# A two-block network on one core: products of zeros in the first stage, half of x scaled before the first split, column tiles in p·V, and reordered queues in four layers

## Chip, core and metric

One core of a Trainium2 chip runs the whole program. The metric is the device time of one execution in microseconds (us), the median of the runs. A profiled execution of the same program gives the trace.

## What is computed

The input x has 256 tokens of 1024 values. A first block and a second block follow each other; every product is of float32 weights with float32 activations. Cut to what matters (`rms_norm_2` is `rms_norm`; rope, gates and residuals are left out where they change nothing in the order of the work):

```python
def first_block(x, ...):
    f = (silu(rms(h) @ w1) * (rms(h) @ w3)) @ w2            # ffn1, width 2816
    h = h + 0.5 * rms_norm(f, ffn1_post_g)
    proj = rms_norm(h, mix_pre_g) @ w_in                    # mix: 10 blocks of columns
    y_a = dsa_attention(q_a, k_a, v_a, q_i, k_i, w_i) @ w_a_out     # 8 heads of 64
    y_b = (gate_b * short_conv_causal(gate_c * conv_in, conv_w)) @ w_b_out
    h = h + rms_norm((sigmoid(g_a) * y_a + sigmoid(g_b) * y_b) @ w_out, mix_post_g)
    h = h + rms_norm(memory_cross_attention(...), xattn_post_g)
    h = h + 0.5 * rms_norm(swiglu(...), ffn2_post_g)        # ffn2
def second_block(x, ...):
    x = x + rwkv7_time_mix(rms_norm(x), ...)                # xx = shift(h) - h; xs = h + xx * mu; r, k, v = xs @ w
    x = x + square(relu(rms_norm(x) @ w1)) @ w2             # mlp1, width 4096
    k, v = shared_kv(x)
    x = x + swa_sink_attention(q, k, v, sinks) @ wo         # window attention, 16 heads of 64
    x = x + square(relu(rms_norm(x) @ w1)) @ w2             # mlp2
```

## The kernel before, in words

The 256 tokens are two tiles of 128 ("token 0" and "token 1" below, `NT` = 2). Activations are kept as columns: a pair of buffers (`XA`, `XB` or `MID`), one with the high and one with the low half of each value. A weight chunk of 128 × 1024 values is loaded by SyncE (SP) into one of six raw slots; ScalarE (ACT) writes its high half (`split_hi`, L263, or L266 where a gain is multiplied in), VectorE (DVE) its low half (`split_lo`, L279 or L282), and TensorE (PE) makes three products of 128 × 128 × 512 for each pair (`product`, L290 to L292: high·high, low·high, high·low). The semaphores `hi_done`, `lo_done` and `chunk_used` tie them: a load waits for the low half that last used its raw slot, a high half waits for the products that last used its split slot. Each engine has one queue, in which the order of all this is written out by hand; `split_hi(A, n)` and `split_lo(V, n)` issue all splits up to chunk n at that place of the queue, and an instruction behind one that waits, waits too.

The layers run one after the other: ffn1, mix, xattn (memory attention), ffn2, time mixing (`tmix`), mlp1, window attention (`window`), mlp2. The feed-forward layers are loops over blocks of their width, with a tail (`pe_tail`) in which the two token tiles go apart, so that the next layer can begin (`follow`).

The places that the change touches:

- *First stage.* `setup.pe` (L1096) waits for the constants and one gain, and transposes the gain (L1099). `pre.turn.pe_token` (L452) transposes x of a token in two groups of four. ACT (`act_token`, L459) and DVE (`dve_token`, L466) write its eight high and eight low columns with the gain multiplied in; `act_deferred` and `dve_deferred` issue the first split ahead of them (`split=1`). A product of chunk m waits for the low half of the chunk and for columns up to 2m + 1. SP issues four chunks, x of token 1 between them, then two chunks that wait for the low halves of chunks 0 and 1, then the small vectors and the constants (L1082 to L633), then the next chunks.
- *p·V.* In `Mix.pe_values` (L1289) and `WindowAttention.pe_values` (L3430) each head's probabilities (128 × 128, plain float32) are the stationary side and 64 columns of values the moving one. A plain float32 call issues two matmuls. `COLUMN_TILES` doesn't exist yet; products that write to half of the partitions are used in the time mixing (L2765, L2813, L2816; L2732 to L2791 use a half of the rows too).
- *Mix.* ACT's exponentials (`act_exp`, L1435) of token 1 are behind `split_hi(A, c[9] + 3)`; the activations before them are sigmoids. In DVE's queue `dve_merge(V, 1)` (L1658) stands behind `split_lo(V, out[1] + 2)`; PE's transposes of the merged rows (L506) wait for it.
- *ffn2's tail and the entry of the time mixing.* `pe_h_turn` (L2417) multiplies h by a diagonal that holds the norm (ACT, L2402). `pe_mixed` starts with the two groups of token 0. ACT: `ffn2_post.act(A, 1)` (Square of the accumulator of token 1, L406), `act_h_cols` (L2284), `act_hi_part` (L2316). DVE: `dve_xx_part` (L2298, L2295), `dve_xs_part` (L2307), `dve_lo_part` (L2312), and between them `ffn2_post.dve_scale` (L656) and `dve_add` (L661). `pe_r_token` waits for the low part of its token and half.
- *Window.* `window.act` and `window.dve` (from L3549 and L3661) interleave the splits with turning h into columns (`act_wide` L487, `dve_wide` L491), the norms, the squares and sums of q (L3513, L3596), q rows (L3604), bias, max and exponentials of four units u (kv group, token), p columns (L3540), o rows (L3654), and the high and low half of o (L3547, L3659). GpSimd (POOL) makes the reciprocal roots (L419, L3364). `WindowAttention.pe` writes out the order of PE: products of q and kv, transposes of q rows (L3398), logits (L3410), transposes of p (L3420), values (L3430), transposes of o (L3439) and the output products (`pe_out`).

## Time and profile before

| | us |
|---|---|
| median of 3 runs | 1415.51 |
| lowest of the runs | 1413.01 |
| the profiled execution: device time | 1416.03 |
| the profiled execution: span of its core | 1414.3 |

In the profile PE is the matmul stream of TensorE and PEld its weight loads, which overlap it; DVE is VectorE, ACT ScalarE, POOL GpSimd, SP SyncE, and SPq SyncE issuing DMAs. A line number is that of the instruction in the kernel; where a helper issues it, that of the helper. "128\*64" behind an operation is rows × columns of the stationary side. A trace can lack a few per cent of the matmul records.

### The profile page before, as it was taken

What the parts mean: (1) busy time and instruction counts of PE and PEld (TensorE: products, weight loads), DVE (VectorE), ACT (ScalarE), POOL (GpSimd) and SP (SyncE); (2) the same over time, 40 slices, a digit from 0 to 9 for tenths busy, and PEclk for the clock granted to TensorE, in tenths of its full rate; (3) what the DMA queues carried; (4) which work ended last, traced back from release to release, by engine and by line L of the source; (5) the groups of instructions that cost most, each with busy time, mean ns of one, the idle gap of its engine ahead of it and who ended that gap; (6) DMA issues with size and microseconds to landing.
All of it is one profiled execution on the core that took longest, in us unless ns stands there. A gap on an engine that the chain in (4) does not pass through costs nothing.

```text
span 1414.3 us, 23277 instructions
## 1 busy us (share of the span) xinstructions
PE 1366.0 (97%) x8675; PEld 1119.8 (79%) x8675; DVE 855.1 (60%) x1235; ACT 697.4 (49%) x1109; POOL 37.7 (3%) x41
## 2 busy tenths in 40 slices
PE   7999999999999999999899999899999988999998
PEld 5888877878788878888677688678888877788887
DVE  4545568875655464455865688656555576565554
ACT  5444456665465554444544453235444456454442
POOL 0000000000000000000000000100000020000000
PEclk9999999999999999999899999999999999999999
DMA  8655546555445565555443100315555641265553
GB/s 290 218 178 178 178 142 209 165 177 194 155 158 161 154 218 192 179 178 179 142 164 98 38 3 32 111 60 179 180 186 184 225 150 45 75 199 188 182 189 104
DMA packets 145534, 220.51 MB, mean 156 GB/s; under 512 B 16760, under 2 KB 65166, under 8 KB 145328
## 3 DMA queue, kind: packets, MB, share of 16 engines
q1 hardware_dynamic: 145456, 219.43, 47.4%
q8 instruction: 54, 0.88, 0.3%
q14 instruction: 24, 0.20, 0.1%
HBM read 218.33 MB, written 1.05 MB: 155 GB/s over the span
## 4 chain that ended last, share of the span: by engine, by line
PE 87%; DVE 6%; ACT 3%; issue 1%; DMA 1%; POOL 1%; SPq 1%; ACTq 0%; DVEq 0%; POOLq 0%
PE acc L290 12%; PE gp L290 12%; PE acc L292 12%; PE acc L291 12%; PE gp L292 12%; PE gp L291 12%; PE gp L2732 1%; PE tp L929 1%; PE acc L2747 1%; DVE sb_w_lo L279 1%; DMA sb_raw<-in_ffn_w 1%; ACT sb_w_hi L263 1%; PE acc L1255 1%; PE tp L290 1%; PE tp L292 1%
## 5 line engine op out<-in xcount | busy, mean ns | idle before, releaser
L279 DVE TENSOR_TENSOR sb_w_lo<-sb_raw,sb_w_hi 128x1024 fp32r<-128x1024 f32 (+1 forms) x380 | 451.7, 1214 | 217.0 <-ACT sb_w_hi L263 215.1
L263 ACT ACTIVATE sb_w_hi<-sb_raw 128x1024 fp32r<-128x1024 f32 (+1 forms) x380 | 388.2, 1053 | 218.2 <-PE acc L292 107.2
L290 PE MATMUL gp<-sb_w_hi,sb_xa_hi 128*128 128x512 f32 (+1 forms) x752 | 301.0, 400 | 11.6 <-DVE sb_xa_lo L2312 6.4
L292 PE MATMUL gp<-sb_w_lo,sb_xa_hi 128*128 128x512 f32 (+1 forms) x752 | 293.8, 391 | 0.0
L291 PE MATMUL gp<-sb_w_hi,sb_xa_lo 128*128 128x512 f32 (+1 forms) x752 | 293.2, 390 | 0.0
L290 PEld LDWEIGHTS gp<-sb_w_hi,sb_xa_hi 128*128 128x128 f32 x752 | 142.5, 190 | 45.3 <-DVE sb_w_lo L279 8.2
L292 PEld LDWEIGHTS gp<-sb_w_lo,sb_xa_hi 128*128 128x128 f32 x752 | 142.4, 189 | 30.1
L291 PEld LDWEIGHTS gp<-sb_w_hi,sb_xa_lo 128*128 128x128 f32 x752 | 142.9, 190 | 27.6 <-issue 0.5
L290 PE MATMUL acc<-sb_w_hi,sb_mid_hi 128*128 128x512 f32 x400 | 156.2, 390 | 0.0
L292 PE MATMUL acc<-sb_w_lo,sb_mid_hi 128*128 128x512 f32 x400 | 155.8, 389 | 0.0
L291 PE MATMUL acc<-sb_w_hi,sb_mid_lo 128*128 128x512 f32 x400 | 155.6, 389 | 0.0
L796 DVE SCALAR_TENSOR_TENSOR sb_arena<-gp,sb_stat,sb_arena 128x256 f32<-128x256 f32 x44 | 19.6, 479 | 131.2 <-ACT sb_arena L773 131.2
L290 PE MATMUL acc<-sb_w_hi,sb_xa_hi 128*128 128x512 f32 (+1 forms) x240 | 95.0, 396 | 3.5 <-DVE sb_w_lo L282 2.0
L773 ACT ACTIVATE sb_arena<-gp,sb_stat 128x256 f32<-128x256 f32 x44 | 18.9, 471 | 148.4 <-PE gp L292 148.4
L292 PE MATMUL acc<-sb_w_lo,sb_xa_hi 128*128 128x512 f32 (+1 forms) x240 | 91.9, 383 | 0.0
L291 PE MATMUL acc<-sb_w_hi,sb_xa_lo 128*128 128x512 f32 (+1 forms) x240 | 91.7, 382 | 0.0
L292 PEld LDWEIGHTS acc<-sb_w_lo,sb_mid_hi 128*128 128x128 f32 x400 | 75.1, 188 | 15.7
L291 PEld LDWEIGHTS acc<-sb_w_hi,sb_mid_lo 128*128 128x128 f32 x400 | 75.1, 188 | 15.4
L290 PEld LDWEIGHTS acc<-sb_w_hi,sb_mid_hi 128*128 128x128 f32 x400 | 75.1, 188 | 15.4
L290 PEld LDWEIGHTS acc<-sb_w_hi,sb_xa_hi 128*128 128x128 f32 x240 | 45.1, 188 | 14.4 <-issue 3.4
L290 PE MATMUL acc<-sb_w_hi,sb_xb_hi 128*128 128x512 f32 x128 | 52.2, 408 | 3.4 <-DVE sb_xb_lo L3659 3.4
L292 PEld LDWEIGHTS acc<-sb_w_lo,sb_xa_hi 128*128 128x128 f32 x240 | 45.1, 188 | 9.1
(409 smaller groups left out, 1751.7 us busy)
## 6 DMA issues: line engine op xcount, KB each, us to landing
sb_raw<-in_ffn_w SPq DMA_DIRECT2D x264, 256.0 KB, 4.3
sb_raw<-in_mlp_w SPq DMA_DIRECT2D x256, 256.0 KB, 2.9
sb_raw<-in_w_in SPq DMA_DIRECT2D x72, 256.0 KB, 3.0
sb_raw<-in_a_w_rkv SPq DMA_DIRECT2D x48, 256.0 KB, 4.3
sb_raw<-in_xattn_w_kv SPq DMA_DIRECT2D x32, 256.0 KB, 3.5
sb_raw<-in_w_out SPq DMA_DIRECT2D x16, 256.0 KB, 2.9
sb_raw<-in_xattn_w_q SPq DMA_DIRECT2D x16, 256.0 KB, 2.9
sb_raw<-in_xattn_w_o SPq DMA_DIRECT2D x16, 256.0 KB, 3.0
```

Source lines behind the costliest of these rows:

```text
L263: A.e.activation(w_hi[:, s, :, 0:n], raw[:, r, :, 0:n], ACT.Copy).then_inc(hi_done, 1)
L279: V.e.tensor_tensor(w_lo[:, s, :, 0:n], raw[:, r, :, 0:n], w_hi[:, s, :, 0:n].bitcast(F32), ALU.subtract).then_inc(lo_done, 1)
L290: e.matmul(dst, xh, wh, start=start, stop=False)
L291: e.matmul(dst, xl, wh, start=False, stop=False)
L292: return e.matmul(dst, xh, wl, start=False, stop=stop)
L773: A.e.activation(self.silu[:, t, 0:256], gp[:, t, 0:256], ACT.Silu, scale=self.norm.st[:, t:t + 1]).then_inc(self.acted, 1)
L796: V.e.scalar_tensor_tensor(self.mid_rows[:, t, 0:256], gp[:, t, 256:512], self.norm.st[:, t:t + 1], self.silu[:, t, 0:256], ALU.mult, ALU. ...
L929: mm = T.e.transpose(tp[:, b, (2 * j + t) * P:(2 * j + t + 1) * P], self.mid_rows[:, t, at:at + P], ident)
L1255: mm = T.e.matmul(self.side(n)[:, j * self.KEYS[t]:(j + 1) * self.KEYS[t]], q, kk, start=True, stop=True)
L2732: mm = T.e.matmul(gp[there, s, m * HALF:(m + 1) * HALF], self.mt[s][at, m, 0, there], self.x_inv[s][at, m, :], start=True, stop=True)
L2747: mm = T.e.matmul(acc[at, s, 512:1024][:, at_m], self.y_inv[s][there, m, :], self.z_buf[s][there, m, :], start=True, stop=True)
```

## The change

One `Exp` of a single column is added, memsets and products of zeros are added in the first stage, `pe_enter` is cut off `pe_mixed` and issued inside ffn2's tail (`follow`, `late=1`), p·V is issued in two column halves, and the rest is a new order of the same instructions. The diff, with the lines around the changes left out:

```diff
@@ -73,6 +73,7 @@
 HALF = P // 2
+COLUMN_TILES = (slice(0, HALF), slice(HALF, P))
@@ -414,7 +415,7 @@
             def pool_token(self, G, t):
-                    G.e.wait_ge(half_ready, 1)
+                    G.e.wait_ge(half_ready, 2)
                     G.e.wait_ge(self.mean, self.count(t))
@@ -452,15 +453,15 @@
-            def act_token(self, A, t, *targets):
-                for k in range(self.kts):
+            def act_token(self, A, t, *targets, ks=None):
+                for k in range(self.kts) if ks is None else ks:
                     A.e.wait_ge(self.turned, self.turned0 + 2 * t + k // 4 + 1)
...
-            def dve_token(self, V, t, *targets):
-                for k in range(self.kts):
+            def dve_token(self, V, t, *targets, ks=None):
+                for k in range(self.kts) if ks is None else ks:
                     V.e.wait_ge(self.hi, self.hi0 + 4 * self.sets * (2 * t + k // 4 + 1))
@@ -577,8 +578,13 @@
                     before0()
-                split_hi(A, first + split)
-                self.turn.act_token(A, 0, *self.targets)
+                if split == 1:
+                    self.turn.act_token(A, 0, *self.targets, ks=range(0, KT // 2))
+                    split_hi(A, first + split)
+                    self.turn.act_token(A, 0, *self.targets, ks=range(KT // 2, KT))
+                else:
+                    split_hi(A, first + split)
+                    self.turn.act_token(A, 0, *self.targets)
                 if before1 is not None:
@@ -592,8 +598,13 @@
                     before0()
-                split_lo(V, first + split)
-                self.turn.dve_token(V, 0, *self.targets)
+                if split == 1:
+                    self.turn.dve_token(V, 0, *self.targets, ks=range(0, KT // 2))
+                    split_lo(V, first + split)
+                    self.turn.dve_token(V, 0, *self.targets, ks=range(KT // 2, KT))
+                else:
+                    split_lo(V, first + split)
+                    self.turn.dve_token(V, 0, *self.targets)
                 if before1 is not None:
@@ -882,7 +893,7 @@
-            def pe_tail(self, T, follow):
+            def pe_tail(self, T, follow, late):
@@ -899,9 +910,11 @@
                     self.columns_ready(T, 1)
+                    if late:
+                        self.pe_down_token(T, i, 1, range(late))
                     if follow is not None:
                         follow()
-                    self.pe_down_token(T, i, 1, range(self.tiles))
+                    self.pe_down_token(T, i, 1, range(late, self.tiles))
                 else:
@@ -939,10 +952,11 @@
-            def pe(self, T, pre, h_ready, acc_free=None, aside=None, turned=True, follow=None):
+            def pe(self, T, pre, h_ready, acc_free=None, aside=None, turned=True, follow=None, late=0):
...
                     pre.turn.pe_token(T, 0, h_rows, h_ready(0))
+                    setup.pe_warm(T, 12)
                 self.pe_up_token(T, 0, 0, range(0, 3), pre.turn)
@@ -961,7 +975,7 @@
                     self.pe_turn(T, i)
-                self.pe_tail(T, follow)
+                self.pe_tail(T, follow, late)
@@ -1094,6 +1108,8 @@
             def pe(self, T):
+                T.e.wait_ge(half_ready, 1)
+                self.pe_warm(T, 8)
                 T.e.wait_ge(consts_loaded, 16)
@@ -1126,7 +1142,15 @@
+            def warm(self):
+                return rows(3)[:, 0, 0:P]
+
+            def pe_warm(self, T, n):
+                for _ in range(n):
+                    T.e.matmul(acc[:, 0, 0:P], self.warm(), self.warm(), start=True, stop=True)
+
             def pool(self, G):
+                G.e.memset(self.warm(), 0.0).then_inc(*G.one(half_ready))
                 G.e.memset(half[:, :], -0.5).then_inc(*G.one(half_ready))
@@ -1286,8 +1310,9 @@
                     for c in range(t + 1):
-                        mm = T.e.matmul(self.side(t)[:, head * HD:(head + 1) * HD], self.p_cols[t][:, c, head, :], self.values[:, c, :],
-                                        start=c == 0, stop=c == t)
+                        for at in COLUMN_TILES:
+                            mm = T.e.matmul(self.side(t)[at, head * HD:(head + 1) * HD], self.p_cols[t][:, c, head, at], self.values[:, c, :],
+                                            start=c == 0, stop=c == t)
                 mm.then_inc(*T.one(self.o))
@@ -1516,7 +1541,9 @@
                 self.act_taken(A, 7, lambda t: rows(5)[:, t, 512:1024], ACT.Sigmoid)
+                A.e.activation(self.sums[:, 8:9], ident[:, 0:1], ACT.Exp).then_inc(*A.one())
                 split_hi(A, c[9] + 3)
+                A.e.wait_ge(*A.last)
                 self.act_exp(A, 1, 0)
@@ -1734,7 +1761,6 @@
                 self.dve_gate_a(V, 1, self.ya1, lambda t: gp[:, t, :])
-                split_lo(V, out[1] + 2)
                 self.dve_merge(V, 1)
@@ -2344,20 +2370,21 @@
                 ffn2_post.dve_mean(V, 1)
+                self.dve_xx_part(V, 0, 1)
+                self.dve_lo_part(V, 0, 0)
                 ffn2_post.dve_scale(V, 1)
-                self.dve_lo_part(V, 0, 0)
                 V.e.wait_ge(*V.last)
                 ffn2_post.dve_add(V, 1)
-                self.dve_xx_part(V, 0, 1)
+                self.dve_xs_part(V, 0, 1)
                 self.pre.rms.dve(V, 1)
-                self.dve_xs_part(V, 0, 1)
                 split_lo(V, r.first[0] + 3)
...
                 split_lo(V, r.first[0] + 4)
-                for g in range(2):
-                    self.dve_xx_part(V, 1, g)
-                    self.dve_xs_part(V, 1, g)
+                self.dve_xx_part(V, 1, 0)
+                self.dve_xs_part(V, 1, 0)
+                self.dve_xx_part(V, 1, 1)
                 self.dve_lo_part(V, 1, 0)
+                self.dve_xs_part(V, 1, 1)
                 self.dve_lo_part(V, 1, 1)
@@ -2444,9 +2471,11 @@
-            def pe_mixed(self, T):
+            def pe_enter(self, T):
                 self.pe_h_turn(T, 0, 0)
                 self.pe_h_turn(T, 0, 1)
+
+            def pe_mixed(self, T):
                 self.pe_r_token(T, 0, 0)
@@ -3427,8 +3456,9 @@
                     for c in range(t + 1):
-                        mm = T.e.matmul(self.o_bank(u)[:, head * HD:(head + 1) * HD], self.p_col[u][:, c, head, :],
-                                        self.kv_rows[:, c, P + kv * HD:P + (kv + 1) * HD], start=c == 0, stop=c == t)
+                        for at in COLUMN_TILES:
+                            mm = T.e.matmul(self.o_bank(u)[at, head * HD:(head + 1) * HD], self.p_col[u][:, c, head, at],
+                                            self.kv_rows[:, c, P + kv * HD:P + (kv + 1) * HD], start=c == 0, stop=c == t)
                 mm.then_inc(*T.one(self.o))
@@ -3439,12 +3469,12 @@
-            def pe_out(self, T, b, t, n):
+            def pe_out(self, T, b, t, n, ms=range(2)):
...
                     T.e.wait_ge(*((self.q_rows, t + 1) if n == 0 else stage(self.o_rows, t + 1)))
-                for m in range(2):
+                for m in ms:
                     c = self.out_first + 4 * b + 2 * n + m
@@ -3493,8 +3523,9 @@
                 self.pe_values(T, 3, (self.o_rows, 3))
-                self.pe_out(T, 1, 0, 1).then_inc(token0_done, 1)
+                self.pe_out(T, 1, 0, 1, range(0, 1))
                 self.pe_turn_o(T, 3, (self.o_done, 3))
+                self.pe_out(T, 1, 0, 1, range(1, 2)).then_inc(token0_done, 1)
                 self.pe_out(T, 1, 1, 0)
@@ -3549,15 +3580,16 @@
                 split_hi(A, self.first + 3)
-                for t in range(NT):
-                    for g in range(2):
-                        self.turn.act_wide(A, t, g, self.entry_bank(t, g), XA)
+                for g in range(2):
+                    self.turn.act_wide(A, 0, g, self.entry_bank(0, g), XA)
                 split_hi(A, self.first + 4)
-                for t in range(NT):
-                    self.rms.act(A, t, h_rows, rows(6)[:, t, :], mlp1_add.h_at(t))
+                self.rms.act(A, 0, h_rows, rows(6)[:, 0, :], mlp1_add.h_at(0))
+                for g in range(2):
+                    self.turn.act_wide(A, 1, g, self.entry_bank(1, g), XA)
+                self.rms.act(A, 1, h_rows, rows(6)[:, 1, :], mlp1_add.h_at(1))
                 split_hi(A, self.kv_first + 2)
                 self.act_squares(A, 0)
-                split_hi(A, q1 + 3)
+                split_hi(A, q1 + 2)
                 self.act_squares(A, 1)
@@ -3578,8 +3610,8 @@
                 split_hi(A, out + 5)
+                self.act_o_hi(A, 1)
                 self.act_p_cols(A, 2)
-                self.act_o_hi(A, 1)
                 self.act_exp(A, 3)
@@ -3667,9 +3699,9 @@
                 mlp1_add.dve(V, 1, mlp1)
+                split_lo(V, self.first + 4)
                 for g in range(2):
                     self.turn.dve_wide(V, 1, g, self.entry_bank(1, g), XA)
-                split_lo(V, self.first + 4)
                 for t in range(NT):
@@ -3677,11 +3709,11 @@
                 split_lo(V, q1 + 1)
+                self.dve_sums(V, 1)
                 self.dve_q_rows(V, 0)
                 split_lo(V, q1 + 2)
-                self.dve_sums(V, 1)
+                self.dve_q_rows(V, 1)
                 split_lo(V, q1 + 4)
-                self.dve_q_rows(V, 1)
                 self.dve_k_sums(V)
@@ -3694,9 +3726,9 @@
                 self.dve_bias(V, 2)
-                split_lo(V, out + 3)
                 self.dve_q_rows(V, 3)
                 self.dve_o_rows(V, 0)
+                split_lo(V, out + 3)
                 self.dve_o_lo(V, 0)
@@ -3838,7 +3870,7 @@
             xattn.pe(T)
-            ffn2.pe(T, ffn2_pre, xattn.post.h_at, xattn.post.freed, None, True)
+            ffn2.pe(T, ffn2_pre, xattn.post.h_at, xattn.post.freed, None, True, lambda: tmix.pe_enter(T), 1)
             tmix.pe_mixed(T)
...
             tmix.pe_core(T)
```

## Rows read from the trace of the kernel before

**Rows 1.** The page: its first line, and the busy time of each engine.
```profile
span 1414.3 us, 23277 instructions
PE 1366.0 (97%) x8675; PEld 1119.8 (79%) x8675; DVE 855.1 (60%) x1235; ACT 697.4 (49%) x1109; POOL 37.7 (3%) x41
```
**Rows 2.** PE's waits, stretches 0:32, 275:365, 675:705, 1130:1225: total, times, longest us.
```profile
PE gp L290 <- DVE sb_xa_lo L466: 3.3, 2, 3.2
...
PE tp L1282 <- ACT sb_arena L1435: 1.6, 1, 1.6
PE tp L506 <- DVE sb_arena L1658: 1.3, 1, 1.3
...
PE gp L290 <- DVE sb_xa_lo L2312: 6.4, 2, 4.5
...
PE acc L290 <- DVE sb_xb_lo L3659: 3.4, 2, 2.0
PE tp L3398 <- DVE sb_arena L3604: 3.3, 2, 1.7
PE acc L290 <- DVE sb_w_lo L282: 2.0, 1, 2.0
```
**Rows 3.** Stretches: length, busy PE PEld DVE ACT POOL (count), clock, DMA, GB/s.
```profile
10.20:12.90 2.70, 2.66 (x6) 1.91 (x7) 2.65 (x8) 2.08 (x3) 0.00 (x0) 1.00 1.10 362
...
29.40:60.00 30.60, 30.60 (x137) 25.01 (x138) 16.34 (x18) 14.41 (x21) 0.00 (x0) 1.00 0.67 220
686.40:692.00 5.60, 5.53 (x14) 4.37 (x15) 4.99 (x12) 2.16 (x4) 0.65 (x1) 0.50 0.83 311
...
699.30:703.00 3.70, 3.70 (x11) 2.92 (x10) 3.44 (x5) 2.37 (x3) 0.00 (x0) 0.54 0.22 70
...
1157.00:1175.00 18.00, 18.00 (x121) 14.77 (x119) 16.05 (x43) 10.88 (x36) 2.99 (x2) 1.00 0.20 68
...
1197.10:1201.50 4.40, 4.32 (x12) 3.43 (x13) 1.43 (x4) 4.25 (x16) 0.00 (x0) 0.61 0.34 106
```
**Rows 4.** The chain that ended last, first stage: start us, us, what.
```profile
8.35 1.22 DVE sb_w_lo L279
9.57 2.07 DVE sb_xa_lo L466 x8
11.64 1.14 DVE sb_w_lo L279
...
18.88 0.66 SPq L240
19.57 7.36 DMA sb_raw<-in_ffn_w
```
**Rows 5.** Timeline of PE, p·V and half-width products: start us, us, engine, line, operation.
```profile
282.64 1.89 PE L1289 MATMUL acc<-sb_arena 128*128 128x64 f32 x16
...
889.01 0.28 PE L2813 MATMUL tp<-sb_arena,sb_shade 128*64 128x64 f32 x4
889.13 0.29 PE L2816 MATMUL tp<-sb_arena,sb_shade 128*64 128x64 f32 x4
...
917.87 0.68 PE L2775 MATMUL acc<-sb_arena,sb_shadow 64*64 64x64 f32 x8
918.47 0.50 PE L290 MATMUL acc<-sb_w_hi,sb_xa_hi 128*128 128x512 f32 x1
```
**Rows 6.** Timeline of ACT, before the exponentials and before the time mixing.
```profile
308.81 1.28 ACT L1435 ACT_TABLE_LOAD   x1
...
678.88 0.40 ACT L2402 ACTIVATE sb_arena<-sb_consts,sb_stat 128x128 f32<-128x128 f32 x1
```
**Rows 7.** The chain that ended last, entry of the time mixing: start us, us, what.
```profile
680.15 0.91 PE tp L2417 x8
...
684.54 1.28 DVE sb_arena L656
...
696.91 1.14 DVE sb_arena L2307 x4
```

## The prediction

> **What bounds the kernel now.** I read the page first: TensorE (PE) is busy 1366.0 of 1414.3 us [rows 1], so nothing that shortens the work of VectorE (DVE), ScalarE (ACT) or a DMA counts unless PE is then waiting for it. Second, PE's waits by stretch [rows 2]: the reader is to see how few there are. The first stage has 3.3 us (longest 3.2), the mix layer 1.6 and 1.3 us, the entry of the time mixing 6.4 us in two waits (longest 4.5), the window layer 3.4 + 3.3 + 2.0 us. The feed-forward loops, most of the span, have none. Third, the pace of PE and its granted clock [rows 3]: undisturbed, 137 products of 512 columns take 30.60 us, 0.223 us each, at clock 1.00. After the waits of the time mixing 14 take 5.60 us at 0.50, and 11 take 3.70 us at 0.54; after one in the window layer 12 take 4.40 us at 0.61. Those are TensorE's two levels, 2.4 and 1.2 GHz, and a wait costs the slow products behind it as well. The stretch 10.2 to 12.9 shows 6 products in 2.70 us, the slow pace, though the row prints a clock of 1.00; I go by the pace. What a new order can win is in these few places.
>
> **The sum is made against the profiled execution**: span 1414.3, device time 1416.03 us. The median of the runs shown is 1415.51, 0.5 lower.
>
> **First stage.** Products of zeros are added (8 before the first transpose, 12 behind token 0's transposes), and ACT and DVE scale half of x before the first split. Before, the chain runs: DVE splits the first chunk from 8.35, makes eight low halves of x from 9.57, and only then splits the second chunk from 11.64; SyncE's issue of a later chunk waits for that split, 13 issues of vectors and constants are behind it in SP's queue, and the chunk issued at 18.88 lands after 7.36 us [rows 4]. PE's stalls around 29 us hang on that landing. With four low halves made before the first raw chunk is split, DVE's 1.22 + 2.07 us of work starts about 0.7 us earlier, so the second split, SP's queue and the landing move by that: −0.7 us. The products of zeros: a plain fp32 product issues two matmuls, 8 + 12 make 40. The first 16 lie under PE's wait for the first DMAs; the other 24 lie between the transposes and the first real product, at 0.11 us each if the clock is up (2.6 us; an estimate from the 0.108 us of L1289 in [rows 5], whose stationary side has the same 128 columns), or twice that if it is not (5.3 us, ending some 2.5 us after the present first product). The memset that they wait for has no row of its size. What the early clock gives, (0.45 − 0.22) × 6 = 1.4 us, is not on the chain that ends last, which is SP's. I take −0.7; bounds −1.5 and +2.
>
> **Column tiles.** p·V in the mix layer (L1289) and the window layer (L3430) is split into two halves of 64 columns. Now 16 such matmuls take 1.89 us, 0.108 us each from start to start; the 24 calls of L1289 and the 48 of L3430 are two matmuls each, 144 in all, 15.6 us [rows 5]. The change makes 288. The same form, 128 rows × 64 columns with 64 moving columns, alternating between the two tiles, stands in the time mixing: four at 889.01, the next at 889.13, 0.029 us each [rows 5]. 288 × 0.029 = 8.4 us, 7.2 less. Entering and leaving a tiled mode: eight matmuls of L2775 at 917.87 hold PE for 0.60 us, against 0.23 at 0.029 each [rows 5]; I take 0.35 for each of the six groups, 2.1 in all (bounds 0 and 0.37 × 6). Net 5.1 us less, of which the two groups in the mix layer, 48 of the 144 with 2 of the 6 switches, are on the path: 5.2 − 2.8 − 0.7 = −1.7 us. The window's share is counted below, without the first group, whose time turns into waiting.
> The Trainium skill (TensorEngine Tiling, "Theoretical Speedup") gives up to 2x where a dimension is at most 64. By it alone the 15.6 us would become 7.8, and the sum would be 0.6 us lower than by the row. Against the change stands the same page's "Key Properties": changing the tiling mode drains TensorE. The 0.60 us row agrees that a switch is not free.
>
> **Mix layer.** The Exp table load of 1.28 us [rows 6] sits in front of the exponentials that PE waits 1.6 us for; a dummy Exp moves it to where ACT waits for PE, one split earlier. ACT's next work there is not needed for two splits: −1.3 us. In the merge, one DVE split (1.22 us, [rows 4] shows one) goes behind the addition that PE waits 1.3 us for; the chunk delayed is three chunks, 8 us of products, ahead of its use: −1.1 us, leaving a rest of 0.2.
>
> **Entry of the time mixing.** The 16 transposing matmuls of token 0 move into the middle of token 1's last 12 down products (6 in front, 6 behind). Now they start at 680.15 by the chain; six products of 0.23 before that is 678.8, but ACT's diagonal is there only at 678.88 + 0.40 [rows 6, 7], so PE waits some 0.5 us there instead. Token 1 of the accumulator is finished 16 × 0.11 + 0.5 = 2.3 us later, and behind it in ACT's queue stands the high half that the first product wants. So I expect the wait of 4.5 us to be cut to about 4.2 by work put into it, and the first product to start at the same time within 0.3 us. The gain comes later: scaling the residual (1.28 us, L656) now stands behind the low part, and the last mix group of token 1 (four of L2307, 1.14 us [rows 7]) now stands behind the low part that PE waits 1.9 us for. About 0.9 us of that wait stays removed after the later start of the residual is taken off. With a wait below 1 us I expect the clock to hold, and 11 products at 0.336 fall to 0.223: 1.2 to 1.6 us. −2.3 us; bounds +2.5 (token 1's delay not hidden) and −4.
>
> **Window layer.** (a) At its entry ACT makes the high half of a chunk and then DVE its low half only after token 1's columns; PE waits 2.0 us. Both orders are turned round, and the chunk is there 4 us before its use: −2.2 with its restart. (b) ACT squares token 1 one split earlier and DVE sums it before it makes q rows 0, so the reciprocal root on GpSimd starts earlier and q rows 1 is there in time: the first of the two L3604 waits goes, −1.9 (the 1.5 and the earlier start of its neighbours). From 1157 to 1175 DVE is busy 16.05 of 18.00 us [rows 3]; it must follow, and every link at its head moves by the same 4.1. (c) A split of 1.22 us [rows 4] leaves the front of q rows 3, of which I take 0.9, because GpSimd's root ends in between; together with the shorter chain to ACT's third p group −1.4. (d) Values 1: 32 matmuls, 3.5 us, become 64, 1.9 + 0.35: −1.2. (e) ACT's high half of o before its p columns, on the chain to the 2.0 us wait: −1.2, and with two waits of 0.6 in place of 2.2 the clock holds, 12 products at 0.367 fall to 0.223: −1.7. (f) Values 2 −0.3, values 3 −1.2. (g) The last output product is cut in two around the transposes of o, so the 1.4 us wait for its low half is under six products: −1.5. Sum 2.2 + 1.9 + 1.4 + 1.2 + 1.2 + 1.7 + 0.3 + 1.2 + 1.5 = 12.6 us. Bounds: 4 (only a and b) and 14 (the waits and slow products of this stretch altogether, plus the tiles).
>
> **Total:** 0.7 + 1.7 + 1.3 + 1.1 + 2.3 + 12.6 = 19.7; 1416.0 − 19.7 = 1396.3, and 1396 against the median.
>
> **The rivals.**
> *The window's second half gives nothing back to PE* (DVE, at 89% from 1157 to 1175, or ACT's exponentials become the wait there). For it: that share. Against it: the waits named are for single links that the new order does shorten. Then only a and b count, 8.5 us less gain: 1405. Chance 0.16.
> *The entry of the time mixing turns worse* because the accumulator of token 1 is late: +2.5 in place of −2.3, 1401. For it: ACT's queue; against: DVE, not ACT, holds the chain at L656. Chance 0.12.
> *More than summed*: the clock also holds at the other two places: 2.5 us at the first wait of the time mixing and 1.3 in the window layer, 1392. Chance 0.08.
> *The column tiles run one behind the other* (the other side). 288 matmuls at the present 0.108 are 31.1 + 2.1 us against 15.6: +17.7; without the tiles' 4.4 the rest of the sum is −15.3, so 1418.4, slower than before. It decides from 0.100 us a matmul. Against it stands the 0.029 row of the same shape. Chance 0.03. A milder form is a floor in PE's sequencer of, say, twice the row, 0.058: 16.7 + 2.1 − 15.6 = +3.2, giving 1404; chance 0.03.
> The Trainium skill (TensorE: Matmul & The Clock Gate, "Wait — 56ns, not 53.3ns?") states such a floor: about 62 ns per MATMUL where hardware decode is off. The 0.029 row speaks against it here; by it the time would be about 1405.
> *The zeros do not lift the clock*: then 24 of them delay the first real product by up to 2.5 us, of which the later waits of that stage take up some; at most +2, 1399, inside the range.
>
> **How the numbers follow.** The forecast has 0.58. Its own width (±4) and the rivals at 1401, 1404 and 1405 are taken in, as is 1392; outside are the slower case and the tails: 1390 to 1408. Two per cent, about what a measurement of this kernel can tell from no change, is 28 us, more than all waits and slow products listed: faster 0.04, slower 0.01, within 0.95.
>
> **What would show it.** The first chunk split on ACT behind four halves of x; products near 10 us at 0.22. L1289 and L3430 with 96 and 192 matmuls at 0.03. No table load in front of the exponentials at 308. L506's wait near 0.2. A wait near 4 us at the entry of the time mixing, the second below 1, clock 1.00 behind it. In the window layer no wait for L282 or before the second L3398; products behind values 1 at clock 1.00. I am wrong if the two window waits reappear under another name, or if the token 1 products of the time mixing start later than now.

## The result, and the profile after

| | before | changed |
|---|---|---|
| median, us | 1415.21 (3 runs, 1413.01 to 1415.51) | 1399.51 (4 runs, 1396.91 to 1400.44) |
| the profiled execution: device time, us | 1416.03 | 1399.79 |
| its span, us | 1414.3 | 1397.6 |

A fourth run of before took 2748.47 us; runs in such a slow state are left out here. The ratio of the times is 0.9894, 95% interval 0.9882 to 0.9906: 1% faster, less than the 2% from which a kernel is called faster here. 1396 was forecast with a range of 1390 to 1408. The median came out 3.5 us above the forecast and inside the range.

The page of the changed kernel, its first line and the busy time, against [rows 1]:

```profile
span 1397.6 us, 23649 instructions
PE 1362.7 (98%) x8859; PEld 1115.1 (80%) x8859; DVE 855.7 (61%) x1235; ACT 697.1 (50%) x1110; POOL 38.1 (3%) x42
```

PE has 184 matmuls more (144 for the halves of p·V, 40 products of zeros) and is still busy 3.3 us less. PE's waits of the changed kernel, stretches 0:32, 275:365, 665:700, 880:915 and 1115:1215 (total, times, longest, us), against [rows 2]:

```profile
PE gp L291 <- DVE sb_w_lo L280: 2.6, 3, 1.4
PE acc L1150 <- POOL sb_half L1154: 1.0, 1, 1.0
...
PE tp L507 <- DVE sb_arena L1685: 0.3, 1, 0.3
PE tp L1306 <- ACT sb_arena L1460: 0.2, 1, 0.2
...
PE gp L291 <- DVE sb_xa_lo L2338: 4.5, 2, 3.6
PE tp L2444 <- ACT sb_arena L2429: 1.7, 2, 1.2
...
PE acc L2747 <- DVE sb_shade L3005: 1.5, 1, 1.5
PE gp L2761 <- issue: 1.0, 1, 1.0
...
PE tp L3427 <- DVE sb_arena L3636: 1.7, 1, 1.7
...
PE tp L3469 <- DVE sb_arena L3686: 0.7, 1, 0.7
PE acc L291 <- DVE sb_xb_lo L3691: 0.5, 1, 0.5
```

The reader is to see: the wait for the exponentials has shrunk from 1.6 to 0.2 and that for the merged rows to 0.3; the wait of 4.5 at the entry of the time mixing is 3.6 now, with a new one of up to 1.2 for ScalarE's diagonal; in the window layer the 2.0 at the entry and one of the two waits for q rows are gone, the other (L3427) stayed at 1.7, and the two waits for the low half of o (3.4 together) have shrunk to one of 0.5. Two lines weren't forecast: a wait of 0.7 for the rows of o (L3469), and a line that I never looked for: 1.0 us that ends on nothing the profile shows, in the core of the time mixing.

Where the gain is, I read by putting the 4704 matmuls of the weight products (512 columns each) in one table, the n-th of before beside the n-th of the other kernel, and taking the difference of their starts. Here are the differences by stretch, for all traces of this study (positive: gained on the first trace of before; places in before's time, us):

| kernel | 0 to 60 | mix layer (to 365) | entry of time mixing (670 to 706) | its core (706 to 930) | window layer (1110 to 1225) | in all |
|---|---|---|---|---|---|---|
| forecast | 0.7 | 4.1 | 2.3 | 0 | 12.6 | 19.7 |
| changed | −0.5 | 4.4 | 2.4 | −1.5 | 11.9 | 16.6 |
| changed_again | 0.1 | 4.3 | 2.4 | −3.0 | 12.3 | 16.2 |
| before_again | 0.4 | 0.0 | 2.8 | 0.2 | 1.6 | 5.0 |
| first_before | 0.6 | 4.4 | 2.4 | −3.4 | 11.8 | 15.9 |
| half_only | 0.9 | 4.4 | 2.4 | −2.3 | 11.9 | 17.3 |
| zeros_only | −0.4 | 4.4 | 2.4 | 0.3 | 12.3 | 18.9 |
| values_in_one | −2.1 | 2.5 | 2.4 | −2.8 | 9.8 | 9.9 |
| window_before | −2.3 | 4.4 | 2.4 | −0.5 | 4.1 | 8.1 |
| entry_before | −0.7 | 4.4 | 3.0 | 0.1 | 10.2 | 16.9 |
| paced | −0.2 | 4.4 | 2.5 | 1.1 | 11.8 | 19.5 |
| best_new_entry | 0.9 | 4.4 | 2.4 | −1.8 | 12.4 | 18.3 |
| best_old_entry | 0.2 | 4.3 | 3.0 | −0.6 | 11.9 | 18.7 |
| mixed_entry | 0.8 | 4.4 | 3.7 | −0.6 | 11.9 | 20.0 |

The row of before_again is the same program as before, traced a second time. It is 5.0 us faster, 4.4 of them in two stretches of the table. That row is why the experiments were needed: a gain read from one pair of traces is partly the luck of the pair.

### The profile page after: what moved, and what is told of

Its sections match the earlier page's. It is cut to its first block, busy times and chain, and to the rows that moved or that the text cites. A ratio compares the mean times of both kernels' runs of the same rounds, so it can differ in the third digit from the quotient of the medians.

```text
span 1397.6 us, 23649 instructions
## 1 busy us (share of the span) xinstructions
PE 1362.7 (98%) x8859; PEld 1115.1 (80%) x8859; DVE 855.7 (61%) x1235; ACT 697.1 (50%) x1110; POOL 38.1 (3%) x42
## 4 chain that ended last, share of the span: by engine, by line
PE 87%; DVE 6%; ACT 3%; issue 1%; DMA 1%; POOL 1%; SPq 0%; POOLq 0%; ACTq 0%; DVEq 0%
PE acc L291 12%; PE acc L293 12%; PE acc L292 12%; PE gp L291 12%; PE gp L293 12%; PE gp L292 11%; PE gp L2761 2%; PE tp L942 1%; PE acc L2776 1%; DVE sb_w_lo L280 1%; DMA sb_raw<-in_ffn_w 1%; ACT sb_w_hi L264 1%; PE acc L1279 1%; PE tp L291 1%; ACT sb_arena L407 1%
## 5 line engine op out<-in xcount | busy, mean ns | idle before, releaser
L280 DVE TENSOR_TENSOR sb_w_lo<-sb_raw,sb_w_hi 128x1024 fp32r<-128x1024 f32 (+1 forms) x380 | 451.8, 1215 | 207.3 <-ACT sb_w_hi L264 205.7
L784 ACT ACTIVATE sb_arena<-gp,sb_stat 128x256 f32<-128x256 f32 x44 | 18.9, 471 | 148.4 <-PE gp L293 148.4
```

The source lines that it names most:

```text
L280: V.e.tensor_tensor(w_lo[:, s, :, 0:n], raw[:, r, :, 0:n], w_hi[:, s, :, 0:n].bitcast(F32), ALU.subtract).then_inc(lo_done, 1)
L784: A.e.activation(self.silu[:, t, 0:256], gp[:, t, 0:256], ACT.Silu, scale=self.norm.st[:, t:t + 1]).then_inc(self.acted, 1)
```

## Experiments

**First stage: first_before, half_only, zeros_only.** The edits, from the changed kernel; first_before makes both, half_only the first alone, zeros_only the second alone:

```diff
-                G.e.memset(self.warm(), 0.0).then_inc(*G.one(half_ready))
-                self.pe_warm(T, 8)
-                    setup.pe_warm(T, 12)
```
```diff
-                if split == 1:
-                    self.turn.act_token(A, 0, *self.targets, ks=range(0, KT // 2))
-                    split_hi(A, first + split)
-                    self.turn.act_token(A, 0, *self.targets, ks=range(KT // 2, KT))
-                else:
-                    split_hi(A, first + split)
-                    self.turn.act_token(A, 0, *self.targets)
+                split_hi(A, first + split)
+                self.turn.act_token(A, 0, *self.targets)
...
```

> The changed kernel with its first stage put back: no memset and no products of zeros, all eight halves of x behind the first split. In the changed kernel the chunk that PE stalls on near 29 us was issued 0.6 us earlier (18.29 for 18.88) and still landed 0.49 us later (27.45 for 26.96), while the DMA engines' share was 0.96 to 1.00 from 20 us on in both. Theory: from 20 us on that stage is bound by the DMA engines and not by the issue, so neither the half of x nor the zeros give anything after 29 us: 1399.0 (0.5 below the changed kernel's 1399.5), first product behind the stall at 29.3. Rival: the issue does set the landing, and the 8.43 us of that one trace was chance: then the old first stage costs the forecast 0.7, 1400.2, product at 30.4 or more. On the side: 40 fewer instructions in PE's queue move the place of the 0.96 us gap at 895.35 (which ends on nothing that the profile shows). If the half clock behind it (898 to 901.5, 1.4 us) hangs on that place, it goes or moves here, and the time is up to 1.4 lower still.

> The changed kernel without its products of zeros (L1150, 16 + 24 matmuls) and their memset; half of x stays in front of the first split. So far: with both parts PE's first products behind the chunk that lands at 27 us start 0.49, 0.74, 0.62 and 0.83 us later than before, and in two of the four traces another 1.46 us is lost between 29.4 and 60 us; with neither part they start 0.60 us earlier than before. Theory: the earlier issue for x-half crowds the DMA queue (the chunk shares it with 0.95 MB of later ones in place of 0.55), so this kernel loses as with both: product near 29.8, time near the changed kernel's. Rival: the zeros do it (their memset, or 40 instructions more to be fetched ahead of PE's first loads): then the product starts 0.6 us before the old 29.33, as with neither, and the time is 1.1 us below the changed kernel's if nothing else moves. In the core of the time mixing 40 instructions fewer put the gap that ends on nothing where first_before has it (2.83 us and 5.6 us of half clock): there it should come out again, since it depends on the count of PE's instructions, so that the total is 1.5 to 2 us above the first-stage forecast.

> The changed kernel with its products of zeros but all eight halves of x behind the first split, as before. Theory (the half of x crowds the queue): product behind the stall near 28.7 to 29.3, no loss. Rival (the zeros do it): product at 29.8 or later. The first six products should run at 0.23 us each in either case, starting near 10.2, since the zeros lift the clock; and the first real product must not be later than before by more than 0.1.

Measured: 1400.69 us (ratio 0.9903, 0.9886 to 0.9920), 1399.20 (0.9891, 0.9868 to 0.9915) and 1399.90 (0.9900, 0.9875 to 0.9924): by time they can't be told apart. The traces tell them apart. The chain that ended last, first stage, of the changed kernel (start us, us, what), against [rows 4]:

```profile
7.79 1.13 DVE sb_xa_lo L467 x4
8.92 1.13 DVE sb_w_lo L280
10.05 1.04 DVE sb_xa_lo L467 x4
11.09 1.14 DVE sb_w_lo L280
...
18.29 0.66 SPq L241
18.99 8.43 DMA sb_raw<-in_ffn_w
```

Up to the issue this pair of traces shows what was forecast: the second split 0.55 us earlier, the issue 18.29 for 18.88. The transfer then takes 8.43 us for 7.36 and eats it. The same line in half_only, and then in zeros_only:

```profile
18.67 7.42 DMA sb_raw<-in_ffn_w
```
```profile
19.22 8.17 DMA sb_raw<-in_ffn_w
```

Over all traces: seven with the zeros take 8.17 to 8.79 us for this transfer, those without them 7.36 to 7.78 (six traces whose chain shows it). So the zeros do it, with the half of x in front or not: of half_only and zeros_only the theory was wrong and the rival right. (For first_before neither held: its product behind the stall starts at 28.7 us, forecast 29.3 or 30.4 and later.) The half of x is shown less clearly: with it the issue is at 17.77 to 18.31 (ten traces, mean 18.1), without it at 18.25 to 18.88 (four traces, mean 18.5), but the two traces of before alone, one program, are 0.49 us apart (18.88 and 18.39). What the zeros bring is there too, the first six products in 1.40 us for 2.66 (timeline of PE, changed kernel: idle time before a group in brackets):

```profile
7.06 2.90 PE L1150 MATMUL acc<-sb_arena 128*128 128x128 f32 x24
10.11 0.50 PE L291 MATMUL gp<-sb_w_hi,sb_xa_hi 128*128 128x512 f32 x1
...
12.27 0.50 PE L291 MATMUL gp<-sb_w_hi,sb_xa_hi 128*128 128x512 f32 x1 [0.51 <-DVE sb_w_lo L280]
```

but PE then waits for splits: at 15 us zeros_only stands about where first_before does, 0.6 and 0.7 us behind the first trace of before. How can 40 products of zeros slow a transfer ten microseconds later? They are 80 instructions of PE (a matmul and a weight load each). DMA queues of the changed kernel, and of half_only, 22 to 24 us (packets, MB, share of 16 engines):

```profile
q1 hardware_dynamic: 177, 0.60, 89.8%
q8 instruction: 1, 0.02, 3.0%
```
```profile
q1 hardware_dynamic: 188, 0.57, 85.9%
```

In every trace with the zeros the first packet of 16 KB of instructions starts between 22.5 and 24.9 us, inside the stretch in which the engines are full with chunks; in every trace without, it comes at 32.4 to 33.4 us, when the chunk has landed. In all fourteen it starts when PE has started 204 to 226 matmuls and weight loads, with the zeros or without: it is PE's own, and the zeros bring PE to that number some 9 us sooner. 3.0% of 16 engines over 2 us is 0.96 us of one engine, and if a chunk counts as landed only with its last part, the delay of one engine is that of the chunk. The size fits the delay of 0.8 to 1.4 us (against 7.36). That the packet comes with the zeros is shown; that it is the packet which delays the chunk, and not something else about the zeros, is argued from the size alone and wasn't tried. In two of the seven, where the wait behind the transfer was longest (1.8 and 1.9 us for 1.3 to 1.6), the clock then fell to 0.50 from 31 to 34 us, which is another 1.46 us lost in values_in_one and window_before.

**p·V in one piece.** 

```diff
-                        for at in COLUMN_TILES:
-                            mm = T.e.matmul(self.side(t)[at, head * HD:(head + 1) * HD], self.p_cols[t][:, c, head, at], self.values[:, c, :],
-                                            start=c == 0, stop=c == t)
+                        mm = T.e.matmul(self.side(t)[:, head * HD:(head + 1) * HD], self.p_cols[t][:, c, head, :], self.values[:, c, :],
+                                        start=c == 0, stop=c == t)
...
```

> The changed kernel with p.V in one piece again (L1313 and L3460: 144 matmuls on 128 columns for 288 on 64). Theory, by the terms of the sum: 1.7 us in the mix layer, 1.2 for values 1, 0.3 and 1.2 for values 2 and 3 come back, 4.4 in all: 1403.9. Rival: only the mix layer's part (trace of the changed kernel: 1.95 us) is on the path, and in the window layer PE waits a little later anyway: 1401.5. Of the half clock behind the gap at 895.35: 96 fewer instructions ahead of it (48 in the mix layer) move it as well; if it hangs on the place it changes here, if it hangs on the 1.49 us wait at 886.6 it stays.

Measured: 1405.91 us, 0.9938 (0.9921 to 0.9956), 2.0 above the theory. In the trace the mix layer loses 1.9 and the window layer 2.1 us against the changed kernel: 4.0, the theory's 4.4 but for the clock. The rest is the two stretches of the table that have nothing to do with p·V: −1.6 in the first stage and −1.3 in the core. Timeline of PE of the changed kernel, against [rows 5]:

```profile
283.18 1.15 PE L1314 MATMUL acc<-sb_arena 128*64 128x64 f32 x32
320.61 2.08 PE L1314 MATMUL acc<-sb_arena 128*64 128x64 f32 x64
...
1177.61 2.09 PE L3460 MATMUL acc<-sb_arena 128*64 128x64 f32 x64
```

About 0.2 of the 2.08 us is the length of the last matmul, so the 64 start 0.030 us apart (an estimate). 16 matmuls at 0.108 and 32 at 0.029 differ by 0.80 us and 0.53 was gained; 32 and 64 differ by 1.60 and 1.38 was gained: by this estimate going over to the half width and back costs 0.2 to 0.3 us (0.35 was taken).

**The window layer's order.**

```diff
-                self.dve_sums(V, 1)
                 self.dve_q_rows(V, 0)
                 split_lo(V, q1 + 2)
-                self.dve_q_rows(V, 1)
+                self.dve_sums(V, 1)
                 split_lo(V, q1 + 4)
+                self.dve_q_rows(V, 1)
...
```
(and likewise the entry, q rows 3, o of unit 1 and the last output product)

> The changed kernel with the window layer's queues put back (entry, q rows 0 and 1, q rows 3, o of unit 1 behind the p columns, last output product in one piece); p.V stays in two halves. Theory: of the 11.8 us that the traces show for the layer the halves of p.V bring 2.7 (1.2 + 0.3 + 1.2), the order 9.1: 1408.6. Rival: order and halves are worth much more together than apart, since a wait that stays long lets the clock fall whatever ran ahead of it: then the order alone is worth all 11 to 12, 1411.

Measured: 1408.07 us, 0.9950 (0.9931 to 0.9969), by the number what the theory says (1408.6). In part that is luck: in its trace 1.8 us are lost in the first stage and 1.0 won in the core against the changed kernel, where nothing was edited. Its waits, 1120 to 1220:

```profile
PE acc L291 <- DVE sb_xb_lo L3689: 3.4, 2, 2.0
PE tp L3427 <- DVE sb_arena L3634: 2.6, 1, 2.6
PE acc L291 <- DVE sb_w_lo L283: 2.0, 1, 2.0
```

In the trace the order is worth 11.9 − 4.1 = 7.8 us, and not 9.1: window_before keeps 2.1 us of gain between 1197.2 and 1203.3, though its wait of 2.0 us is back. There the first trace of before has half clock ([rows 3], 0.61), and neither window_before nor before_again has. And it loses 0.95 us just before, of which more below. before_again, clock of the 4.3 us behind its wait of 2.02:

```profile
1193.70:1198.00 4.30, 4.26 (x25) 3.72 (x26) 1.40 (x3) 4.22 (x16) 0.00 (x0) 1.00 0.33 103
```

**The entry of the time mixing: entry_before and before_again.** entry_before puts back the place of the transposes and VectorE's order:

```diff
-            ffn2.pe(T, ffn2_pre, xattn.post.h_at, xattn.post.freed, None, True, lambda: tmix.pe_enter(T), 1)
+            ffn2.pe(T, ffn2_pre, xattn.post.h_at, xattn.post.freed, None, True)
...
-                self.dve_xx_part(V, 0, 1)
-                self.dve_lo_part(V, 0, 0)
                 ffn2_post.dve_scale(V, 1)
+                self.dve_lo_part(V, 0, 0)
...
```

> The changed kernel with the entry of the time mixing put back (transposes of token 0 of h behind the last down products, old order of VectorE's pieces). Theory: the entry is worth what the two traces show between 678 and 706 us, 2.25 us, and the loss of 1.4 us between 894 and 906 has nothing to do with it: 1401.8, with the second wait on L2338 back near 1.9 us and the granted clock near 0.5 behind it. Rival: the entry moved the phase of everything behind it and so brought the loss; then the loss goes with it: 1400.4.

> The kernel before, unchanged, for a second trace. In entry_before the code of the entry is that of before, and yet 3.0 us of gain appear between 670 and 706 us: half clock for 3.3 us behind the first wait and none behind the second, where the first trace of before has 7.6 and 3.6 us. If the length of such a stretch is a matter of the single execution, this second trace shows other lengths than 7.6 and 3.6, and the same for the 0.80 us gap at 900.3. If it belongs to the program (its timing up to there is the same each time), they come again within 0.3 us.

Measured: entry_before 1399.10 us, 0.9889 (0.9872 to 0.9906), no slower than the changed kernel, where the theory had 1401.8 and the rival 1400.4. Both its waits are those of before, and the clock isn't. Waits 670 to 705 and two stretches (clock is the third number from the end):

```profile
PE gp L291 <- DVE sb_xa_lo L2338: 6.5, 2, 4.5
...
682.90:686.00 3.10, 3.10 (x8) 2.48 (x9) 2.53 (x6) 1.15 (x2) 0.38 (x1) 0.52 1.04 385
693.70:697.40 3.70, 3.67 (x16) 3.06 (x17) 3.37 (x4) 3.44 (x5) 0.00 (x0) 1.00 0.10 22
```

before_again (one run, 1411.03 us) shows the same, 1.00 behind its second wait of 1.9 us:

```profile
697.10:700.80 3.70, 3.70 (x16) 3.07 (x17) 3.43 (x4) 3.43 (x4) 0.00 (x0) 1.00 0.09 22
```

So behind equal waits of 1.9 us the clock fell in one trace (0.54, [rows 3]) and held in three (best_old_entry too). Against those three the new entry gains nothing: 2.4 us in all nine traces that have it, where the old one has 2.8, 3.0 and 3.0. The Trainium skill (TensorE: Matmul & The Clock Gate, "What's actually happening") says that the window in which the clock's monitor looks at the engine runs freely and doesn't start with the kernel. The two traces of before agree with it as far as they go: the same program, behind the same wait, fell in one (0.54) and not in the other (1.00). What phase it had no trace shows.

**Paced loads.** One line, at the end of SP's queue of the time mixing:

```diff
                 for c in range(self.out.first[0] + 6, self.out.end):
                     load_chunk(sp, c)
+                sp.wait_ge(self.y_done, 2 * self.GROUPS - 1)
```

> The changed kernel with one wait more in SP's queue: the first eight loads of mlp1 (2 MB) wait until the last but one group of y of the time mixing is in its rows (about 901 us), in place of being issued from 887.7 on. In all six traces PE has one gap here that ends on nothing the profile shows (0.68 to 2.83 us), and in each a packet of instructions of 16 KB starts 1.5 to 2.7 us before the gap's end, 9.5 us after the one before it, where others are 4 to 5 us apart; in between the DMA engines' share is 0.9 to 1.0 with these loads. Theory: PE's instructions are fetched behind the loads; without them the gap goes, the packets come 4 to 5 us apart, and the clock holds between 897 and 902: 1399.5 - 0.96 - 1.4 = 1397.1. Rival: the gap has another cause (it stays, 1399.5), or the 1.49 us wait before it is what lets the clock fall (gap gone, half clock stays: 1398.5). Against it: the loads, now 13 us later, might come late for mlp1's first products near 930.

Measured: 1397.78 us, 0.9882 (0.9858 to 0.9906), 1.7 below the changed kernel (2.4 were expected). The two weren't timed side by side and their ranges overlap (1396.60 to 1399.08 against 1396.91 to 1400.44), so the time alone shows nothing. The trace does: the gain of the core is 1.1 in place of −1.5. What the changed kernel has there, timeline of PE and clock:

```profile
894.91 0.44 PE L2761 MATMUL gp<-sb_shadow,sb_shade 64*64 64x64 f32 x7
896.31 0.45 PE L2761 MATMUL gp<-sb_shadow,sb_shade 64*64 64x64 f32 x9 [0.96 <-issue]
...
888.00:895.30 7.30, 6.93 (x223) 6.23 (x224) 5.34 (x15) 1.91 (x5) 0.00 (x0) 1.00 0.96 328
898.00:901.60 3.60, 3.60 (x59) 3.44 (x56) 2.05 (x4) 0.38 (x1) 0.00 (x0) 0.53 0.02 6
```

and the waits of paced from 880 to 912, with no such line:

```profile
PE acc L291 <- DVE sb_xa_lo L492: 1.5, 1, 1.5
PE acc L2748 <- DVE sb_shade L3006: 1.5, 1, 1.5
```

PE is at 61 instructions per us before the gap (223 matmuls, 224 loads in 7.3 us), a block of 256 in 4.2 us, and the packets of 16 KB come about that far apart, 4 to 5 us. Around the gap they don't. The DMA queues of the changed kernel from 884.6 to 893.6 us, and from 893.7 to 894:

```profile
q1 hardware_dynamic: 1187, 2.48, 81.4%
...
q1 hardware_dynamic: 53, 0.10, 97.8%
q8 instruction: 1, 0.02, 20.2%
```

Nine microseconds without a packet of instructions, while SP's twelve loads hold the engines at 0.96 (888 to 895.3), and the gap ends 2.3 us behind the start of the late one (893.97). In paced the two packets start at 883.87 and 891.08, 7.2 us apart and not 9.7. Two more things tie the gap to PE's fetches. In all thirteen traces that have it, it ends 2.3 to 2.6 us behind the start of the late packet, whatever its length. And counted from the start of the program it begins each time behind the 12466th or the 12722nd of PE's matmuls and weight loads, which are 256 apart, in kernels whose instructions in front of it differ by up to 176. (best_old_entry has one more such gap, 0.42 us ending at 832.3, behind the 9650th, eleven times 256 sooner.) The Trainium skill (Runtime: NRT & Kernel Launch, "Instruction fetch mechanics") has blocks of 16 KiB and 256 instructions, which these packets bear out, and calls the cost of crossing one mostly hidden: here it isn't, at 0.5 to 2.8 us a time, with 3.4 or 6.8 us of half clock behind it in six of the thirteen traces.

**Together: best_new_entry, best_old_entry, mixed_entry, changed_again.** All four were timed side by side. The first three have no zeros and the paced loads; the second has the old entry, the third this mixture:

```diff
-            ffn2.pe(T, ffn2_pre, xattn.post.h_at, xattn.post.freed, None, True, lambda: tmix.pe_enter(T), 1)
+            ffn2.pe(T, ffn2_pre, xattn.post.h_at, xattn.post.freed, None, True)
...
             def pe_mixed(self, T):
+                self.pe_enter(T)
```

> The changed kernel without its products of zeros and with the paced loads of mlp1. The traces so far: six with the zeros have the transfer that PE stalls on in the first stage at 8.17 to 8.79 us, four without at 7.36 to 7.42, and a 16 KB packet of instructions at 23 to 25 us in the six, at 32 to 33 in the four; paced took the gap near 896 away, with the clock at 1.00 behind it. Theory: both add up. Paced is 1397.8; without the zeros 1.1 less: 1396.7, first product behind the stall near 28.5, no gap between 888 and 908. Rival: 40 instructions fewer move the fetches so that a gap comes back somewhere else: 1398 to 1399.

> As best_new_entry, and the entry of the time mixing as before (transposes of token 0 of h behind the last down products, old order of VectorE). Counted from before's second trace, the first product behind the second wait came 0.4 to 0.6 us sooner with the old entry (two traces) than with the new (seven traces, all at one time within 0.1), as long as the half clock behind the first wait is short. Theory: the new entry is worth nothing or less: 1396.3, 0.4 below best_new_entry. Rival, the forecast's: the new entry is worth about 2, 1398.7.

> As best_new_entry, with the transposes of token 0 of h behind the last down products as before, but VectorE's pieces in the new order (low part ahead of the scaling of the residual, last group of token 1 behind its low part). With the new place of the transposes token 1 of the accumulator is done 2.4 us later (ScalarE's square at 679.02 for 676.62), and behind it the root of token 1 (VectorE's add at 683.79 for 682.88), the diagonal (687.96 for 686.31) and the high part of token 0's second half. Theory: the place of the transposes costs what the order of VectorE wins. With the order alone the low part is ready behind ScalarE's high part of 680.21 + 0.63, so the first product starts 1.4 us earlier, and the low part of token 1 one group of 1.14 us earlier: 1.4 below best_old_entry, 1394.9. Rival: the scaling behind the low part delays token 1 by as much: equal to best_old_entry within 0.4.

> The changed kernel, unchanged, for a second trace and more runs beside the others. The deterministic part should come again within 0.1 us at each place (entry of the time mixing 2.4 between 670 and 706, window layer 11.4 to 11.8), the transfer of the first stage above 8.1 us; free to differ are the length of the half clock behind the first wait of the time mixing (3.3 to 7 us so far), the 1.46 us at half clock between 29 and 60 (two of five traces with both parts of the first stage), the half clock behind the gap near 896, and that near 1170. Median 1399.5 if the first runs were typical.

| | median, us | range | ratio (95%) |
|---|---|---|---|
| best_new_entry | 1397.67 | 1397.18 to 1399.62 | 0.9885 (0.9870 to 0.9900) |
| best_old_entry | 1398.35 | 1397.65 to 1401.55 | 0.9893 (0.9876 to 0.9909) |
| mixed_entry | 1396.69 | 1396.38 to 1397.70 | 0.9878 (0.9861 to 0.9894) |
| changed_again | 1400.18 | 1398.86 to 1401.07 | 0.9898 (0.9883 to 0.9913) |

mixed_entry is the best kernel of the study, 3.5 us below the changed one beside it, with ranges that don't meet. All three best kernels are 1.0 to 2.1 us above what was expected of them (1396.7, 1396.3, 1394.9). Against best_old_entry mixed_entry is 1.7 us lower (1.4 expected), but there the ranges meet by 0.05 us, and the traces differ by 1.3, of which 0.6 are in the first stage, where both have the same code. In its trace the first product of the time mixing starts 1.3 us earlier than with the old place and old order, as expected (1.4); of that 0.6 are left at 706, which is also 1.2 us earlier than with the new entry. Its waits, 670 to 705:

```profile
PE gp L291 <- DVE sb_xa_lo L2335: 4.2, 2, 3.3
PE tp L2441 <- ACT sb_arena L2426: 0.3, 1, 0.3
```

Between best_new_entry and best_old_entry times don't decide (the ranges overlap); the traces have the old entry 0.6 us ahead in this stretch (3.0 against 2.4). The rival of best_new_entry came true: its gap is back, as it is in the other two.

```profile
PE acc L2777 <- issue: 1.7, 1, 1.7
```

Without the zeros PE's blocks begin at other instructions. The late fetch then falls on SP's loads of `in_a_g` and of the last two chunks of the output weights (packets at 879.18 and 889.83 in best_new_entry), and the paced loads come only behind those. What the paced loads still gain is the length of the gap: 1.7, 1.2 and 1.5 us in the three, 2.6 and 2.8 in half_only and first_before. And changed_again repeats the mix layer and the entry within 0.1 us (the window layer has 0.4 more, since the clock held behind L3427), while the core is at −3.0 for −1.5: the same program, a gap of 1.23 for 0.96 us and then 6.8 us of half clock for 3.4.

## Why the prediction was right, and where it was wrong

The 19.7 us of the sum were 16.6 in the pair of traces: 3.4 us are missing in three stretches, and 0.4 came on top in the two others.

*First stage (0.7, measured −0.5).* The step that failed is "SP's queue and the landing move by that". The issue moved (0.6 us in this pair, 0.4 in the mean of all traces). The landing doesn't follow where the zeros are: the transfer takes 8.43 us for 7.36. I had put the zeros at no cost because what they give is "not on the chain that ends last". I counted their time on PE (2.90 us for 24, forecast 2.6) and that of their memset, and not that their instructions have to be fetched by the same DMA engines that the stage is short of. Without the zeros, the traces with the half of x have a gain of 0.2 to 0.9 us at 60 us, those without it 0.0 to 0.6: about 0.3 in the mean, and less than what two traces of one program differ by.

*The core of the time mixing (not in the sum, measured −1.5, and −3.0 in the second trace).* The trace of before had it, an "issue" of 0.8 us at 900.34, and I never asked what it was. No edit touches this code. The gap is there in every trace but one, at one of two numbers in PE's count of instructions, hence its place and its length depend on edits anywhere.

*Window layer (12.6, measured 11.9).* (a) 2.3 and (b) 1.7 came as forecast (2.2, 1.9), (g) 1.35 for 1.5, (e) 1.5 for 1.2 (against window_before), (f) 0.6 and 1.4 for 0.3 and 1.2, and the clock 1.55 for 1.7. Two terms were too large. (c) gave 0.9, and 1.3 where the clock held behind it, for 1.4. The wait at L3427 was to shrink and stayed at 1.7: what the order took from it, the shorter first group of p·V put back, as values_in_one shows, where this wait is 0.9. (d) gave 0.65 for 1.2. The group itself is 1.6 us shorter, but PE then stands 0.73 us at the transposes of o, where it didn't stand before, and 0.95 of the 1.6 is gone again; window_before, with the new p·V and the old order, shows the same 1.6 and the same loss, and values_in_one, with the old p·V, neither. So the step that failed in (d) is the one that put all of the shortening on PE's path; behind this group VectorE's rows of o are the bound. The 1.7 for the clock came, but it was booked as a gain of the change, and before_again has 1.55 of it with nothing changed.

*The mix layer (4.1, measured 4.4)* is right by each of its terms: p·V 1.9 for 1.7, the table load 1.4 for 1.3, the merge 1.0 for 1.1. Of the table load and the merge that is read from traces; no run puts them back alone. The rival of tiles that run one behind the other and that of a floor of 0.058 us are refuted by 0.030.

*Entry of the time mixing (2.3, measured 2.4).* The number is right by luck. The waits came as forecast (3.6 for 4.2, and 0.9, below 1), and so did the start of the first product, but they were not worth what was forecast. Of the 2.4, 1.3 lie between 700 and 706 and are the half clock behind the second wait of before's first trace; before_again and entry_before, with the old order, have them too. Against these the new entry loses 0.4 to 0.6 us. The rival "accumulator of token 1 late" is what the traces show, at a fifth of its price (+2.5): ScalarE's square starts at 679.02 for 676.62 in entry_before, the diagonal of token 1 at 687.96 for 686.31, and PE has the new wait for it. What VectorE's order wins, mixed_entry shows: 1.3 us at the first product, 0.6 at 706.

*The base.* The sum started from 1416.03. Over 26 runs of before in this study the median is 1413.7 (1411.03 to 1418.78), over nine of the changed kernel 1399.8. The profiled execution of before lies 2.3 us above that median; its clock fell behind two waits behind which it held in before_again. The difference of the medians is 13.9 us, where the two profiled executions differ by 16.2. That 1396 was missed by only 3.5 us is in part errors that cancel: about 3 us of returned clock were in the sum, and the half clock that they were to remove was in the base. From 1413.7 the same 19.7 us would have given 1394.

## What to carry to other kernels

Take two traces of the kernel before when the terms of a sum are near 1 us. What differs between them, above all half clock behind a wait, is no gain that an edit can claim; only the wait itself is. A shorter group on one engine is worth only what the next wait doesn't take back. An "issue" gap in a stretch of short matmuls beside heavy loads is worth a look at the instruction packets in the DMA queues. Instructions that fill idle time on PE are not free where DMA is the bound. When an edit moves work and changes an order at once, try the two apart: here, at the end of the stretch, the order won 0.6 us and the move lost 1.2.

## What the runs showed of the hardware

- The granted clock printed 1.00 from 10.2 to 12.9 us in before, while products went at 0.45 us ([rows 3]); with zeros in front they go at 0.23 under the same 1.00. The trace's record of the clock only begins at 13.3 us in before, where its products go over from 0.43 to 0.23 us from start to start, and at 7.2 us in the changed kernel; what a view prints for earlier is not a reading. Over all traces it begins at 5.0 to 7.2 us with the zeros and at 13.3 to 15.9 without.
- Instructions come in 16 KB packets on a DMA queue of their own (q8). PE ran dry for 0.5 to 2.8 us where loads held the engines at about 1 and the packet came late, always 2.3 to 2.6 us before PE went on and always at the same place in a block of 256 of its matmuls and weight loads. And a transfer took 8.17 to 8.79 us in the traces in which such a packet fell beside it, and 7.36 to 7.78 in those in which none did; that the packet is the cause there is not shown.
- Behind the same wait of 2.02 us the clock fell once and held twice; behind one of 4.54 us (old entry) it stayed at half for 6.8, 3.4, 3.4 and 3.4 us.
- Half-width plain float32 matmuls of 64 columns on alternating tiles start 0.030 us apart, and going over to them and back costs an estimated 0.2 to 0.3 us.
